# Strassen's seven products of half blocks for 19 of 22 stripe pairs of a feed-forward input product

## What is computed

```python
a, bgate = jnp.split(rmsnorm(x, g_ffn[l]) @ w_ffn_in[l], 2, axis=-1)
x = x + (jax.nn.silu(a) * bgate) @ w_ffn_out[l]
```

## Time and profile before

| | |
|---|---|
| median of three runs | 1533.83 us |
| the profiled execution | 1533.16 us |
| its span, first to last instruction | 1531.4 us |
| mean granted TensorE clock | 0.993 |
| feed-forward block, from its first to its last chunk | about 765 to 1519 us |

### The profile page before, as it was taken

How to read it: one execution, slowest core, us unless ns; L and a number is a source line. 1 busy time by engine, 2 the same in 40 slices (tenths; PEclk the granted TensorE clock), 3 DMA queues, 4 the chain that set the end, 5 groups by cost and what they waited for, 6 DMA issues and landing times.

```text
span 1531.4 us, 24255 instructions
## 1 busy us (share of the span) xinstructions
PE 1496.1 (98%) x9703; PEld 1457.2 (95%) x9703; DVE 771.1 (50%) x1305; ACT 321.8 (21%) x471; POOL 382.7 (25%) x349
## 2 busy tenths in 40 slices
PE   7999999999999999999999999999999999999998
PEld 7998998979999988789999999999999999999998
DVE  5215477678753287557845444333444422344434
ACT  4021334361120134310031111101111101111111
POOL 2122146135531161125521110001111000111163
PEclk9999999999999999999999999999999999999999
DMA  5311300101151265221111111111111111111113
GB/s 161 108 41 42 96 28 22 49 21 42 55 152 42 83 214 199 100 94 42 55 42 43 53 41 46 51 41 56 41 41 55 42 54 43 42 53 57 41 42 111
DMA packets 155018, 101.12 MB, mean 66 GB/s; under 512 B 9508, under 2 KB 147748, under 8 KB 154947
## 3 DMA queue, kind: packets, MB, share of 16 engines
q1 hardware_dynamic: 154955, 100.24, 21.6%
HBM read 91.50 MB, written 8.96 MB: 66 GB/s over the span
## 4 chain that ended last, share of the span: by engine, by line
PE 92%; DVE 5%; ACT 1%; issue 1%; POOL 1%; SPq 0%; DMA 0%; DVEq 0%; ACTq 0%; POOLq 0%
PE pm L1670 27%; PE pm L1672 27%; PE pm L1671 27%; PE pm L1996 2%; PE pm L1923 2%; PE pm L2021 1%; PE pm L1787 1%; POOL st L660 1%; PE pm L1816 1%; DVE b L1246 0%; PE pm L1984 0%; PE pm L1789 0%; DVE proj L1335 0%; DVE S L1283 0%; PE pm L2086 0%
## 5 line engine op out<-in xcount | busy, mean ns | idle before, releaser
L1670 PE MATMUL pm<-x_hi,w_hi 128*128 128x344 f32 x1728 | 557.2, 322 | 2.6 <-DVE w_lo L1161 2.3
L1671 PE MATMUL pm<-x_lo,w_hi 128*128 128x344 f32 x1728 | 552.5, 320 | 0.0
L1672 PE MATMUL pm<-x_hi,w_lo 128*128 128x344 f32 x1728 | 552.3, 320 | 0.0
L1670 PEld LDWEIGHTS pm<-x_hi,w_hi 128*128 128x128 f32 x1728 | 325.3, 188 | 5.4 <-DVE w_lo L1161 2.6
L1671 PEld LDWEIGHTS pm<-x_lo,w_hi 128*128 128x128 f32 x1728 | 325.1, 188 | 0.2
L1672 PEld LDWEIGHTS pm<-x_hi,w_lo 128*128 128x128 f32 x1728 | 325.3, 188 | 0.0
L646 POOL TENSOR_TENSOR raw<-raw,gains 128x1024 f32<-128x1024 f32 x72 | 137.5, 1911 | 689.0 <-DMA raw<-in_w_ffn_in 564.0
L845 ACT ACTIVATE w_hi<-raw 128x1024 fp32r<-128x1024 f32 x120 | 127.2, 1060 | 847.2 <-PE pm L1672 778.0
L1670 PE MATMUL pm<-s_hi,w_hi 128*128 128x344 f32 x528 | 169.0, 320 | 0.0
L1671 PE MATMUL pm<-s_lo,w_hi 128*128 128x344 f32 x528 | 168.7, 319 | 0.0
L1672 PE MATMUL pm<-s_hi,w_lo 128*128 128x344 f32 x528 | 168.6, 319 | 0.0
(11 more groups left out here) (269 smaller groups left out, 1966.0 us busy)
## 6 DMA issues: line engine op xcount, KB each, us to landing
raw<-in_w_ffn_in SPq DMA_DIRECT2D x44, 512.0 KB, 3.8
raw<-in_w_in SPq DMA_DIRECT2D x20, 512.0 KB, 3.7
vc<-in_cache_mem_v SPq DMA_DIRECT2D x16, 512.0 KB, 3.9
raw<-in_w_ffn_out SPq DMA_DIRECT2D x16, 512.0 KB, 4.1
xt<-in_x_prompt SPq DMA_DIRECT2D x8, 512.0 KB, 5.9
raw<-in_w_out SPq DMA_DIRECT2D x8, 512.0 KB, 4.2
raw<-in_w_cq SPq DMA_DIRECT2D x8, 512.0 KB, 4.1
vc<-in_cache_mem_k SPq DMA_DIRECT2D x8, 512.0 KB, 5.5
```

Source lines behind the costliest of these rows:

```text
L1670: pe.matmul(out, w_hi[s][:, k, :], hi[:, k, x0:x0 + cols], start=(k == 0), stop=False)
L1671: pe.matmul(out, w_hi[s][:, k, :], lo[:, k, x0:x0 + cols], start=False, stop=False)
L1672: last = pe.matmul(out, w_lo[s][:, k, :], hi[:, k, x0:x0 + cols], start=False, stop=(k == kb - 1))
```

## The change

The feed-forward input product is made in one go, before any `down`. Its 22 pairs are now 2 classical pairs (stage `in0`, "head"), 19 pairs by seven products, and one classical pair (`TAIL`).

For a pair of stripes the 2 x 2 blocks are: of the weights, a or b by the even or odd one of each two of the 8 contraction blocks (4 blocks each, `KP`); of the tokens, even or odd blocks by the first or second half of the 516 tokens (`HALF`). Seven products of 4 contraction blocks by 516 tokens, in two chunks of 258 (`Q`), take the place of eight. This is the variant of Winograd with shared sums. The operands are four weight blocks as they are and three sums, on the token side four blocks of sums, made once (`token_sums`, half by GpSimd and half by VectorE, in the head), and split into `th` and `tl`. The products go into 8 banks in turn. VectorE adds each to one of six kept partial results (`part`), 14 additions a pair, of which eight give rows a (`ga`) and b (`gb`). GpSimd scales the two rows by `rb`, ScalarE takes the Silu, VectorE multiplies (`row_product`), and SP stores the row in DRAM (`s_rows`). The 22 rows come back in four groups of 4, 4, 8 and 6, are split by ScalarE and VectorE (`group_hi`, `group_lo`), and each `down` waits for the split of its whole group. The `down` stages are four instead of three, their matmuls as many as before. In the head ScalarE's eight copies of token sums (`token_hi`) come behind the Silu chunks of the first pair, and ahead of the split of the fourth stripe.

The diff, cut to its core:

```diff
-GROUPS = ((0, 8), (8, 8), (16, 6))
+GROUPS = ((0, 4), (4, 4), (8, 8), (16, 6))
+HEAD = 2
+PAIRS7 = FB - HEAD - 1
+HALF = T // 2
+Q = HALF // 2
+KP = KB // 2
...
-    for f0, fb in GROUPS:
-        ph += [Phase(f"in{f0}", 2 * fb, NC, 2), Phase(f"down{f0}", 8, NC, None)]
+    ph += [Phase("in0", 2 * HEAD, NC, 2), Phase(f"in{FB - 1}", 2, NC, 2)]
+    ph += [Phase(f"down{f0}", 8, NC, None) for f0, fb in GROUPS]
...
+        th = [put(f"th{n}", [P, 2, 4, HALF], F32R, at=(r0 + 18 * Z, r0)[n]) for n in range(2)]
+        tl = [put(f"tl{n}", [P, 2, 4, HALF], F32R, at=(r0 + 22 * Z, r0 + 4 * Z)[n]) for n in range(2)]
+        raw7 = [put("raw_c", [P, 2, KB, P], at=g2), raw]
+        wh7 = [w_hi[n // 2][:, KP * (n % 2):KP * (n % 2 + 1), :] for n in range(4)]
...
+        part_a = put("part_a", [P, 2, Q], at=g2 + 30784)
+        part_b = put("part_b", [P, 4, Q], at=r2 + Z)
+        part = [part_a[:, n, :] for n in range(2)] + [part_b[:, n, :] for n in range(4)]
...
+            def pairs_of_seven(p):
+                sp.wait_ge(mm_done, p.done)
+                for s in range(2):
+                    load_pair(0, 0, s)
+                sp.wait_ge(fprod, NC)
+                store_row(0, 0, gb[0])
+                for s in range(2):
+                    sp.wait_ge(lo_made, p.first + 3 + s)
+                    load_pair(0, 1, s)
+                sp.wait_ge(fprod, 2 * NC)
+                store_row(1, 1, gb[1])
+                def body(i, par):
+                    sp.wait_ge(wl7_made, lin(i, par, 7, 6))
+                    if isinstance(i, int) and 2 * i + par == PAIRS7 - 2:
+                        for s in range(2):
+                            load_stripe(TAIL, 0, s, False)
+                    elif not (isinstance(i, int) and 2 * i + par > PAIRS7 - 3):
+                        for s in range(2):
+                            load_pair(i + 1, par, s)
+                    if late(i, par, 1):
+                        sp.wait_ge(row_made, lin(i, par, 1, 0))
+                        store_row(lin(i, par, 1, HEAD - 1), 1 - par, gb[1 - par])
+                sevens(sp, body, PAIRS7 - 3)
+                sp.wait_ge(prod_done, 14 * PAIRS7)
+                load_row(0)
+                load_row(1)
+                sp.wait_ge(row_made, PAIRS7)
+                store_row(FB - 2, 0, gb[0])
+                load_row(2)
+                load_row(3)
+            def load_row(f):
...
+            def load_groups(p):
+                fs = {"down0": (4, 5, 6, 7), "down4": tuple(range(8, 16)), "down8": tuple(range(16, 22)), "down16": ()}[p.name]
+                per = -(-len(fs) // 2)
+                for i in range(p.stripes // 2):
+                    for s in range(2):
+                        load_stripe(p, i, s)
+                    if i == 0 and p.name == "down0":
+                        sp.wait_ge(fprod, 3 * NC)
+                        store_row(FB - 1, 1, fb_last)
+                        sp.wait_ge(quad_made, 14 * PAIRS7)
+                        sp.wait_ge(row_out[0], ROW_OLD[0] + 16 * 11)
+                    if i == 0 and p.name == "down4":
+                        sp.wait_ge(acc_made, 8 * NC)
+                    if i == 0 and p.name == "down8":
+                        sp.wait_ge(mm_done, p.done)
+                    if i < 2:
+                        for f in fs[i * per:(i + 1) * per]:
+                            load_row(f)
...
+        def token_sums(eng, made, n):
+            ks = 4 * n
+            def block(odd, half):
+                cols = slice(half * HALF, (half + 1) * HALF)
+                return (x_hi[:, ks + odd:ks + 4:2, cols].bitcast(F32), x_lo[:, ks + odd:ks + 4:2, cols].bitcast(F32))
...
+            eng.wait_ge(made, OLD + 7)
+            eng.tensor_tensor(out[3], tmp[2], out[1], ALU.subtract).then_inc(made, 1)
+            yield
...
+            def weight_sums(i, par):
+                r = raw7[par]
+                a11, a12, a21, a22 = r[:, 0, 0::2, :], r[:, 0, 1::2, :], r[:, 1, 0::2, :], r[:, 1, 1::2, :]
+                g = gains[:, 2, :].unsqueeze(2).to_broadcast([P, KB, P])
+                for s in range(2):
+                    pool.wait_ge(raw7_in[par][s], OLD + 16 * (i + 1))
+                    pool.tensor_tensor(r[:, s, :, :], r[:, s, :, :], g, ALU.mult).then_inc(gain7_on, 1)
+                pool.wait_ge(gain7_on, OLD + lin(i, par, 2, 2))
+                if late(i, par, 1):
+                    pool.wait_ge(prod_done, lin(i, par, 14, 8 - 14))
+                else:
+                    pool.wait_ge(mm_done, ph["in0"].done + 6 * HEAD)
+                pool.tensor_tensor(sum3, a11, a21, ALU.subtract).then_inc(sums_made, 1)
+                pool.wait_ge(sums_made, lin(i, par, 4, 1))
+                pool.tensor_tensor(sum2, a22, sum3, ALU.subtract).then_inc(sums_made, 1)
+                pool.wait_ge(sums_made, lin(i, par, 4, 2))
+                if late(i, par, 1):
+                    pool.wait_ge(wl7_made, lin(i, par, 7, 0))
+                pool.tensor_tensor(sum4[:, :, :], a12, sum2, ALU.subtract).then_inc(sums_made, 1)
+                pool.tensor_tensor(a21, a21, a22, ALU.add).then_inc(sums_made, 1)
+            def rows_scaled(i, par):
+                pool.wait_ge(quad_made, lin(i, par, 14, 14))
+                pool.tensor_tensor(ga[:, :], ga[:, :], rb[:, :], ALU.mult).then_inc(row_scaled, 1)
+                pool.tensor_tensor(gb[par][:, :], gb[par][:, :], rb[:, :], ALU.mult).then_inc(row_scaled, 1)
+            def in_head(p):
+                pool.wait_ge(stored, 16 * 5)
+                pool.wait_ge(xl_made, 16 * NC)
+                steps = token_sums(pool, t_pool, 0)
+                for n in range(5):
+                    next(steps)
+                for s in range(2):
+                    gain_stripe(p, 1, s)
+                for n in steps:
+                    pass
+                weight_sums(0, 0)
+                def body(i, par):
+                    if late(i, par, 1):
+                        rows_scaled(i if par else i - 1, 1 - par)
...
+                sevens(pool, body)
+                rows_scaled((PAIRS7 - 1) // 2, (PAIRS7 - 1) % 2)
...
+            def token_hi(n):
+                for q in range(4):
+                    act.wait_ge((t_pool, t_dve)[n], OLD + 8)
+                    act.activation(th[n][:, :, q, :], tlf[n][:, :, q, :], ACT.Copy).then_inc(th_made, 1)
+            def weight_hi(i, par, n):
+                if late(i, par, 1):
+                    act.wait_ge(prod_done, lin(i, par, 14, 2 * n + 2 - 14))
+                elif n < 4:
+                    act.wait_ge(mm_done, ph["in0"].done + (9, 9, 12, 12)[n])
+                if n in (0, 1, 4):
+                    act.wait_ge(gain7_on, OLD + lin(i, par, 2, 2 if n == 4 else 1))
+                else:
+                    act.wait_ge(sums_made, lin(i, par, 4, {3: 1, 2: 2, 6: 3, 5: 4}[n]))
+                act.activation(wh7[n], weight_part(par, n), ACT.Copy).then_inc(wh7_made, 1)
+            def silu_rows(i, par):
+                act.wait_ge(row_scaled, lin(i, par, 2, 1))
+                act.activation(ga[:, :], ga[:, :], ACT.Silu).then_inc(row_silu, 1)
+            def in_head(p):
+                for i in range(HEAD):
+                    split_next(p, i, 0, i == HEAD - 1)
+                    if i == 0:
+                        norm_factors(2)
+                    for c in range(NC):
+                        silu_chunk(p, i, c, ga)
+                        if c == 1 and i < HEAD - 1:
+                            split_next(p, i, 1, False)
+                    if i == 0:
+                        token_hi(1)
+                        token_hi(0)
+                for n in range(7):
+                    weight_hi(0, 0, n)
+            def seven(i, par):
+                if late(i, par, 1):
+                    weight_hi(i, par, 6)
+                for c in range(2):
+                    act.wait_ge(prod_done, lin(i, par, 14, 1 + c))
+                    if late(i, par, 1):
+                        act.wait_ge(quad_made, lin(i, par, 14, 4 - 14))
+                    act.activation(part[c], bank[c][:, 0:Q], ACT.Copy).then_inc(part_made, 1)
+                if late(i, par, 1):
+                    silu_rows(i if par else i - 1, 1 - par)
+                if isinstance(i, int) and 2 * i + par == PAIRS7 - 1:
+                    for s in range(2):
+                        act.wait_ge(prod_done, 14 * (PAIRS7 - 1) + 4 * s + 4)
+                        split_hi(TAIL, 0, s, None)
+                else:
+                    for n in range(6):
+                        weight_hi(i + par, 1 - par, n)
...
+            def down_weights(p):
+                for i in range(p.stripes // 2):
+                    last = i == p.stripes // 2 - 1
+                    split_next(p, i, 0, last)
+                    split_next(p, i, 1, last)
+                    for f in NEXT_GROUP[p.name][i]:
+                        group_hi(f)
...
+            def token_lo(n, q):
+                dve.wait_ge(th_made, OLD + 4 * (1 - n) + q + 1)
```

(98 more changed lines are left out.)

221 lines of the change are left out of this document (173 added, 48 removed).

## The result

The changed kernel takes 1524.2 us (median, 1523.5 to 1524.9) against 1533.6: a ratio of 0.9939 [0.9927, 0.9951], 9.4 us less. The forecast was 1514 with a range of 1499 to 1524. The sign was right, the size was less than half of it, and the time lies 0.2 us outside the range. The profiled execution took 1524.86 us, span 1523.0, so the spans differ by 8.4 us.

What follows compares the result with a forecast made beforehand. TensorE, busy in 98% of the span with matmuls, was taken as the bound; -46 + 14 + 3 + 6 + 3 = -20 us on the profiled 1533.2 gave 1513, adjusted to 1514 for the median, range 1499 to 1524.

Steps and rivals of the forecast that it cites:

- Price of a matmul: In the 19 seven-product pairs: 168 matmuls at 120.4 ns replace 144, 20.22 us for 22.65, so 46 us less.
- The head: Two classical pairs ahead: stripe (1,1) starts 14 us late, plus 3 us at the head's end; bounds 4 and 22.
- The end: Output stages: splits of returned rows leave holes of 2.2 and 2.8 us before groups two and three; 6 us in all.
- rival 3: Output stages: row loads push weights back in two groups and the first group's split is late; +8, 1522 us, chance 0.12.
- The least margin is 4 us, so I take 0 for the 19 pairs: In the 19 pairs, VectorE and GpSimd finish at least 4 us before TensorE needs them, so no time is added.
- Two or three such falls: 3 us: Clock falls behind the head's holes of 3 to 7 us cost 3 us, bounds 0 and 6.
- rival 4: In the 19 pairs, more frequent bank changes lower the clock for a tenth of them; +32 us, 1546 us, chance 0.02.
- Rival 1: In the 19 pairs, VectorE and GpSimd bind through their port, about 1.1 us more a pair; 1537 us at worst, chance 0.07.
- Rival 2: The head is covered, costing 4 us instead of 17, and no clock falls; 1499 us, chance 0.13.

Runs made afterwards that it cites:

- experiment 1: Against the changed kernel, ScalarE splits the head's fourth stripe, (1,1), ahead of its eight copies of token sums; 1515.8 us, ratio 0.9886.
- experiment 9: Against the changed kernel, GpSimd begins its token sums only when VectorE's first three are made; 1522.4 us, ratio 0.9922.
- experiment 7: Against the changed kernel, GpSimd scales only 8 of the 1032 columns of each row, so the result differs; 1516.4 us, ratio 0.9885.
- experiment 8: Against the changed kernel, GpSimd scales row b a second time in every pair, so the result differs; 1574.1 us, ratio 1.026.
- experiment 3: Against the changed kernel, VectorE makes the last pair's two low parts for the next stage behind its first additions, not ahead; 1519.9 us, ratio 0.9919.
- experiment 2: Against the changed kernel, VectorE makes one token sum instead of three ahead of its first evacuation, the others later; 1527.4 us, ratio 0.9958.

## Why the prediction was right in sign and wrong in size

**Price of a matmul** (-46 forecast). Right: 119.7 ns against 120.4, and without the round's drag 20.15 us a pair against 20.22. That is -47.5 for the nineteen.

**The head** (14 + 3 forecast). Right in sum, and the place and cause of the hole before stripe (1,1) too (experiment 1): 817.67 for 815, holes of 17.2 us together. What I had missed was a hole of 6.5 us before the first eviction. I had given GpSimd 1.8 us a turn, and VectorE's three sums ahead of its evictions little more than their own 1.1; a turn is 3.3 to 3.4. The hole before stripe (1,1), forecast as 14, was 5.7, since 6.5 + 0.4 + 1.1 were paid before it. That its start came so near is in part luck. From 774.23 to 807.56, where VectorE's last token sum ends, 33.3 us pass, for 32 forecast as full turns; with the measured times of the operations alone (seven sums of 2.46 and four gains of 1.90 on GpSimd, eight sums of 1.23, a low part, two products and five evictions on VectorE) full turns would be an estimated 39. Operations priced too short and an overlap left out made up for each other. The page "SBUF — State Buffer" of the Trainium skill (Two separate sides) says that the pair of ports is locked for a whole instruction; experiment 9 agrees but for the 0.3 us by which a turn is shorter than the sum of both.

**The end** (6 forecast). Right: 5.8 us, at the two turns named, 2.46 and 3.05 for 2.2 and 2.8. No row load held a matmul back, so rival 3 is out.

**"The least margin is 4 us, so I take 0 for the 19 pairs"** failed. First, GpSimd's sizes: a scaling of 1032 columns takes 2.41 to 2.79 us where 1.9 was taken from the gain, whose second operand is a broadcast, and a sum 1.3 to 1.6 for 1.05 to 1.15. "GPSIMD Engine Reference" of the Trainium skill (Elementwise — side-by-side cycle accounting) has 4497 ns for a two-input add of 2048 columns; scaled to 1032 columns that is an estimate of 2.27. The trace's 2.41 lies nearer to it than to my 1.9; no run here has 2048 columns. Second, I measured the margin inside one pair from its first matmul, and did not follow the wait for the last addition on into the next pair; so I never saw that the round closes without TensorE. Experiments 7 and 8 settle this: take 4.4 us of scaling away and the pairs come to 20.15, add 2.41 and all of it appears. The margin of 4 us was there at the start, but it was one supply for all nineteen pairs: at 0.25 to 0.3 us a pair it was gone after thirteen. The last pair, with two more operations in it, was not worked out by itself at all. Term: 0 forecast, 4.7 measured (3.3 and 1.4), and the fall behind it.

**"Two or three such falls: 3 us"** was the largest miss: six, 9.9 us. I had looked at holes of 3 to 7 us alone. The traces of the experiments show that shorter holes count too, though not each time. The same hole of 2.46 us at the first turn, in two kernels (windows; columns as in the earlier trace rows), first of experiment 1, then of experiment 3:

```profile
1289.30:1293.30 4.00, 4.00 (x16) 4.00 (x17) 0.41 (x1) 0.00 (x0) 0.00 (x0) 0.57 0.93 350
```

```profile
1291.60:1295.60 4.00, 4.00 (x25) 4.00 (x26) 1.65 (x2) 0.00 (x0) 0.00 (x0) 1.00 0.92 342
```

Clock 0.57 in the one, 1.00 in the other. The granted clock is at the lower level, 1.2 GHz, in part of the first stretch and at 2.4 GHz in the whole second. In the feed-forward block of the twelve kernels and the change, all the holes of 3.6 us and more were followed by a fall; of those of 1.8 to 3.5 us some were and some not; none of 1.7 us or less was. A fall cost 1.1 to 2.6 us. In the pairs, where the products change banks every 12 matmuls, the clock was 1.00. So rival 4, the bank cycling of "TensorE: Matmul & The Clock Gate" (the second failure mode) of the Trainium skill, did not come about; what cost clock was plain holes.

Rival 1 named the right mechanism for the drift at the wrong size (1.1 us a pair for 0.25, and that in the last five only). Rival 2, a covered head, is out: the head's holes are 17.2 us where it had 4. The upper end of the range was a slip besides: the bounds that it names, 22 for the head and 6 for the clock, add up to 1522 and not 1524. The sum with the measured terms is -47.5 + 17.2 + 5.8 + 4.7 + 9.9 = -9.9 for the forecast's -46 + 17 + 6 + 0 + 3 = -20.

## What to carry to other kernels

When two engines work for a third, follow their waits once round, from an operation to the same operation a period later, and compare that length with the third engine's period: a margin inside one period only says after how many periods the difference shows, here thirteen. Price a hole of TensorE with the fall of the clock that may follow, 1.1 to 2.6 us here; four small reorderings of queues, none of which removed work, were worth 22 us, more than twice the change itself. Four orders of the token sums moved the head's first holes and left the time; whether taking work off GpSimd and VectorE there would shorten the head is not tested. Look into the trace before the edited place, too: most of the 3 us of experiment 2 lay 400 us ahead of its edit.

## What the runs showed of the hardware

- GpSimd's two-operand operation on 1032 columns takes 2.41 to 2.47 us by itself; VectorE's takes 1.23 for the same operands. Side by side both take 3.3 to 3.4.
- Equal holes have unequal prices. In the kernel of experiment 8, with a hole of 1.9 us in most pairs, TensorE ran at 1.00 behind the hole at 936.49 and at 0.61 behind the same one at 959.38:

```profile
936.50:940.50 4.00, 4.00 (x33) 4.00 (x34) 4.00 (x8) 0.00 (x0) 3.76 (x3) 1.00 0.33 132
959.40:963.40 4.00, 4.00 (x22) 4.00 (x23) 4.00 (x8) 0.00 (x0) 3.76 (x3) 0.61 0.33 132
```

  What tells the two apart is left open. It makes a difference of single microseconds between two kernels of this kind uncertain: 2.9 of the 7.8 us of experiment 7 were of this sort.
